# Where TensorE's dense pieces stand in the HGRN head: five of 32 moved behind the norm sum

## The reference, cut to what matters

```python
proj = u @ P['w_in'][l]                       # columns for A, B, C and the gates G
# HGRN2, per head, chunk by chunk
o_inter = jnp.einsum('bhtk,bhkv->bhtv', q_c * jnp.exp(g_cum), s)
att = jnp.einsum('bhtk,bhsk,bhtsk->bhts', q_c, k_c, dec)
o = o_inter + jnp.einsum('bhts,bhsv->bhtv', att, v_c)
s = jnp.exp(g_last)[:, :, 0, :, None] * s + jnp.einsum('bhsk,bhsv->bhkv', k_c * jnp.exp(g_last - g_cum), v_c)
# after all chunks
o = o * lax.rsqrt(jnp.mean(o * o, axis=-1, keepdims=True) + RMS_EPS) * norm_g
out = o * jax.nn.silu(gz)
# merge
ga, gb, gc = jnp.split(jax.nn.sigmoid(pg), 3, axis=-1)
merged = ga * (oa @ proj_a) + gb * (ob @ proj_b) + gc * (oc @ proj_c)
```

## Time and profile before

| | |
|---|---|
| median of three runs | 2198.53 us (2196.08 to 2199.20) |
| the profiled execution | 2198.53 us, span 2196.7 us |
| mean granted TensorE clock | 0.993 |
| TensorE busy, matmuls | 2106.6 us, 96% |
| VectorE, ScalarE busy | 1311.3 us, 817.7 us |
| HGRN heads in the span | about 647 to 773 us and 1728 to 1854 us |

### The profile page before, as it was taken

The page is one execution under the profiler, slowest core; times in us unless marked ns, Lnnn a source line. Parts: engine busy times, 40 slices in busy tenths (PEclk is TensorE's granted clock), DMA queues, the critical chain, the costliest instruction groups (busy, mean ns, idle before and its releaser), DMA issues.

```text
span 2196.7 us, 30927 instructions
## 1 busy us (share of the span) xinstructions
PE 2106.6 (96%) x12624; PEld 1856.3 (85%) x12624; DVE 1311.3 (60%) x1947; ACT 817.7 (37%) x931; POOL 35.9 (2%) x72
## 2 busy tenths in 40 slices
PE   5999999999999989999999999999999999999998
PEld 5999997777766688999989998977777666989998
DVE  4664376776556674665366644766764576656643
ACT  3554352122143144554355534412112323445532
POOL 0000000000000000000000000000000000000000
PEclk9999999999999999999999999999999999999999
DMA  4444421111132242444434443211111323324442
GB/s 167 153 153 156 170 96 45 68 49 68 44 107 106 100 154 96 146 148 159 160 137 148 150 160 134 102 39 51 67 54 65 111 107 127 137 96 152 152 155 100
DMA packets 38067, 252.13 MB, mean 115 GB/s; under 512 B 4720, under 2 KB 4912, under 8 KB 9424
## 3 DMA queue, kind: packets, MB, share of 16 engines
q1 hardware_dynamic: 33120, 234.60, 30.1%
q0 software_dynamic: 4848, 16.13, 2.0%
HBM read 242.05 MB, written 8.67 MB: 114 GB/s over the span
## 4 chain that ended last, share of the span: by engine, by line
PE 85%; DVE 8%; ACT 2%; DVEq 2%; issue 1%; DMA 1%; ACTq 0%; POOLq 0%
PE dps L580 42%; PE dps L532 15%; PE dps L487 9%; DVE tmp L1203 2%; PE mx L680 2%; PE mx L674 2%; PE mx L682 2%; ACT tmp L891 1%; PE mx L549 1%; PE mx L560 1%; PE mx L487 1%; PE mx L789 1%; DVEq L1632 1%; PE mx L825 1%; DVE ho L1203 1%
## 5 line engine op out<-in xcount | busy, mean ns | idle before, releaser
L532 PE MATMUL dps<-u,raw 128*128 128x320 f32 x1536 | 478.0, 439 | 0.0
L1200 DVE TENSOR_TENSOR wlo<-raw,whi 128x2048 fp32r<-128x2048 f32 x136 | 311.7, 2292 | 259.9 <-ACT whi L891 254.9
L580 PE MATMUL dps<-uh,whi 128*128 128x320 f32 x1408 | 433.2, 308 | 34.7 <-DVE wlo L1200 25.5
L580 PE MATMUL dps<-uh,wlo 128*128 128x320 f32 x1408 | 436.0, 310 | 0.0
L580 PE MATMUL dps<-ul,whi 128*128 128x320 f32 x1408 | 434.7, 309 | 0.0
L891 ACT ACTIVATE whi<-raw 128x2048 fp32r<-128x2048 f32 x138 | 262.8, 1905 | 389.4 <-PE dps L580 380.5
L532 PEld LDWEIGHTS dps<-u,raw 128*128 128x128 f32 x1536 | 269.5, 190 | 89.2 <-issue 13.7
L580 PEld LDWEIGHTS dps<-uh,whi 128*128 128x128 f32 x1408 | 266.4, 189 | 37.6 <-issue 31.2
L580 PEld LDWEIGHTS dps<-ul,whi 128*128 128x128 f32 x1408 | 265.6, 189 | 1.3 <-issue 0.2
L580 PEld LDWEIGHTS dps<-uh,wlo 128*128 128x128 f32 x1408 | 266.5, 189 | 0.0
L580 PE MATMUL dps<-hfh,whi 128*128 128x320 f32 x704 | 221.1, 314 | 0.0
(11 more groups left out here) (297 smaller groups left out, 3026.1 us busy)
## 6 DMA issues: line engine op xcount, KB each, us to landing
raw<-in_wstream SPq DMA_DIRECT2D x220, 1024.0 KB, 4.8
hs<-in_st_hgrn POOLq DMA_DIRECT2D x8, 512.0 KB, 6.2
out_o_hgrn<-hs POOLq DMA_DIRECT2D x8, 512.0 KB, 2.9
sw<-in_smallw POOLq DMA_DIRECT2D x2, 1024.0 KB, 5.2
ss<-in_st_rwkv POOLq DMA_DIRECT2D x8, 256.0 KB, 3.9
out_o_rwkv<-ss POOLq DMA_DIRECT2D x8, 256.0 KB, 2.3
x<-in_xT SPq DMA_DIRECT2D x4, 320.0 KB, 4.3
out_yT<-x SPq DMA_DIRECT2D x4, 320.0 KB, 2.2
```

What stands on the lines that cost most here:

```text
L532: m = pe.matmul(dps[:, 2 * s + c, 0:T], w[:, k, c * P:(c + 1) * P], u[:, k, :], start=k == 0, stop=k == KD - 1, skip_group_check=True)
L580: m = pe.matmul(dps[:, 2 * half + c, 0:T], w[:, k, c * P:(c + 1) * P], v[:, k0 + k, :], start=first and k == 0 and i == 0, stop=last and k ...
L1200: return nc.vector.tensor_tensor(out, a, b, op)
```

## The change

Of the 32 pieces of each head, the five that stood singly or in a pair between the state products and the end of the output products are issued at the end of the head, behind the norm sum. The number of pieces, their order among themselves, and every wait and semaphore are as before. The 17th piece, the first of the second block, now comes behind `o_done`.

```diff
                 pe.matmul(mx[:, 2, P:2 * P], kt3[:, 1, :], vt3[:, 1, :], start=True, stop=True)\
                     .then_inc(S["hst1_done"], 1)
-                dense_part(1)
                 pe.wait_ge(S["hb_ready"], n + 1)
                 for j in range(2):
                     m = pe.matmul(mx[:, j, :], kt3[0:CH, 2, :], hvb[0:CH, 4 * j:4 * j + 4, :], start=True, stop=True)
                 m.then_inc(S["hst_done"], 1)
-                dense_part(2)
                 pe.wait_ge(S["hst1_ready"], n + 1)
                 pe.wait_ge(S["hs_loaded"], n * 16 + 16)
...
                 for b in range(NB):
-                    if b % 4 == 0:
-                        dense_part(1)
                     t0 = TP + b * TS
                     m = pe.matmul(mx[:, 3, t0:t0 + TS], hs[:, b, :], qps[1][:, t0:t0 + TS], start=False, stop=b == NB - 1)
                 m.then_inc(S["o_done"], 1)
                 dense_part(3)
                 pe.wait_ge(S["osq_ready"], n + 1)
                 pe.matmul(mx[:, 2, 0:T], ones, osq, start=True, stop=True).then_inc(S["om_done"], 1)
-                dense_part(8)
+                dense_part(13)
```

## The result

The changed kernel takes 2209.74 us (median of 4 runs, 2209.49 to 2210.34) against 2197.33 before (4 runs, 2196.08 to 2199.20): a ratio of 1.0056, 95% interval 1.0039 to 1.0074. It is slower by 12 us. Measured once more in a later comparison it took 2207.89 against 2198.16, 1.0042 (1.0026 to 1.0057). The profiled execution took 2208.12 us with a span of 2206.3, 9.6 us more than before, so that is what the traces have to account for.

The account below looks back on a forecast made before the run. It took TensorE's queue length plus its few waits to bound the kernel. Pace 0, new waits 0, first wait -2.1, second wait +2.1 and clock +1.6 on 2198.5 gave 2200.1 us, range 2195.8 to 2202.4.

Parts of the forecast that it names:

- The clock at that pause: Pause behind the fourth heads: both pauses become the longer kind, one more clock fall than now, +1.6 us.
- a sign of being wrong: Distance from head to head: a change of over 0.3 us would show the prediction wrong.
- the one on the slower side: L794 becomes a wait if VectorE's chain is over 0.62 us later; 2203.1 us at 1.2 later; chance 0.05.
- The pace: Each head: 2.60 to 2.98 us saved in the stretch against 2.69 added at the end; taken as 0.
- the lower of the two readings of the 0.10: Stretch from L784: the 0.10 us after a change of rows stays without the pieces, so it is not saved.
- The waits that come closer: Ahead of L789 and L794: 0.48 and 0.62 us of cover left, so no new wait, cost 0.
- What comes earlier: `o_done` and its chain come 2.7 us earlier; VectorE's lead ends waiting at L1614, so nothing is gained.
- The last head: Behind the fourth head: first wait of 1.05 us goes, third half's grows from 2.37 to 3.42; gain 0.
- 1: Behind the last head: first wait goes, second grows, layer 1 keeps its clock; 2198.5 us; chance 0.36.
- 2: Behind the last head: the 1.05 us gain is kept in each layer; 2196.4 us; chance 0.05.
- 3: Level loop: VectorE's lead carries through five later levels of each head, saving 15 us; 2184 us; chance 0.04.
- 4: Ahead of L794: VectorE's chain comes later than its 0.62 us cover; 2203.1 us at 1.2 later; chance 0.05.

Follow-up runs that it names:

- e7: Changed kernel's order plus an unread identity-times-constants product in each of the five gaps, against the kernel before: 2219.98 us against 2197.74, ratio 1.0095.
- e5: Kernel before with the five pieces moved behind `o_done` but ahead of the norm sum: 2204.52 us against 2197.74, ratio 1.0034.
- e8: Kernel before with the five pieces moved into levels 3 to 6 and ahead of L779: 2195.89 us against 2197.74, ratio 0.9988.
- e1: Kernel before with the change made only in the fourth head of each layer: 2202.48 us against 2198.15, ratio 1.0025.
- e2: Kernel before with the change made only in the first three heads of each layer: 2203.91 us against 2198.15, ratio 1.0028.
- e9: Kernel before with three pieces, from ahead of L789, L794 and L783, moved into levels 4 to 6: 2189.50 us against 2197.74, ratio 0.9960.
- e3: Kernel before with only the two single pieces around L802 moved to the head's end: 2202.08 us against 2198.15, ratio 1.0023.
- e6: Kernel before with all five pieces in one clump between L789 and L794: 2203.89 us against 2198.16, ratio 1.0026.
- e4: Kernel before with only the three pieces ahead of L794 moved to the head's end: 2201.67 us against 2198.15, ratio 1.0021.
- e11: Second measurement of the kernel with three pieces moved into levels 4 to 6, against the kernel before: 2186.07 us against 2198.16, ratio 0.9942.
- e10: Three pieces in levels 4 to 6, the one left ahead of L794 moved ahead of the first L802, against the kernel before: 2187.69 us against 2198.16, ratio 0.9951.

## Why the prediction was wrong

*The step that failed is the one named "The clock at that pause".* It asked for the clock only where TensorE stands still, and took it as given, 1.00, inside the heads. There it fell in four of eight, 1.7 us each, 6.8 us in the profile, and these heads came 1.7 us further apart, where the prediction had named 0.3 as a sign of being wrong. The rule of the Trainium skill that I leaned on (TensorE: Matmul & The Clock Gate, "What's actually happening": the slow state is the default, activity releases it) speaks of activity, and I read it as the absence of pauses. The trace speaks against my reading: in the window ahead of the fall shown above TensorE is busy throughout. It does not speak against the rule's wording, and e7, where added wide products take most of the falls away, agrees with it. No rival had it either; the one on the slower side was a wait.

*In the same step, the size at the pause was too small.* I forecast one fall more, +1.6. Measured from steps in the profile, the two places lose 3.8 us more: both have a fall, as forecast, and each lasts longer than the one fall before the change (0.72 over 12 us against 0.86).

The other steps held. *The pace:* the stretch from L784 to the dense row took 7.96 us and takes 5.27, so taking the pieces out saves 2.69 a head, exactly what they cost at the end; 31.35 us a head against 31.36 before, so 0, as the lower of the two readings of the 0.10 had it: L788 to L792 is 1.91, L798 follows L795 0.36 us behind, the 0.10 behind a change of rows stays. *The waits that come closer:* no idle ahead of L788 or L792. *What comes earlier:* VectorE's lead ends in its wait at L1614 of before:

```profile
682.09 0.44 DVE L1610 COPY_PREDICATED ho<-cst,mx 128x256 f32<-128x256 uint32 x1 [2.83 <-PE mx L768]
```

2.83 us against 0.15, forecast 2.8; the level loop gained nothing. *The last head:* first wait gone, second one at 3.63 against 3.42 forecast, gain kept 0; the chain starts at the last piece. *The rivals:* 1 falls with the clock, 2 with the second wait, 3 with the wait at L1610, 4 since L792 follows at once. The sum of the parts other than the clock was 0 and measured 0; the whole error is the clock inside the heads and the size of its falls behind them.

That the falls come from the stretch without dense pieces is shown by the runs together. The bare stretch brings them without the longer pause and the long row (e5), a wide product in each gap takes them from four to one with the order of the change kept (e7), and a kernel with the stretch bare behind full levels has them in every head (e8). Over all profiles, heads with the bare stretch hold a fall in 25 cases of 40 (both profiles of the changed kernel, e1, e2, e5, e8), heads with their pieces as before in none of 16 (before, e1, e2). And all 35 falls in heads, those behind a pause left out, begin between 0.8 us ahead of the last small product's start and 1.2 us behind it. What is not shown is which products of the stretch count how much: with some of the pieces in it there are falls in three heads, two, one or none of eight (three in e9, two in e3 and e6, one in e4 and e11, none in e10).

## What to carry to other kernels

Wide instructions between small matmuls may be holding the clock and not hiding a wait, so before they are moved out of a thin run, look at what is left of the run and, afterwards, at the granted clock in windows of a few us behind it: the page's slices average a fall away, and a busy TensorE says nothing. If such work is to be moved, the profitable place is where TensorE waits for another engine (0.54 us of work put into a level cost 0.03 here), and enough of it has to stay behind: five pieces moved there gained nothing clear of noise, three gained 8 to 12 us.

## What the hardware showed that I had not expected

The granted clock fell to 1.2 GHz with TensorE 3.00 of 3.00 us busy ahead of the fall, after products of 128, 512 (64 rows), 64 and 8 columns. Products of the identity with constants in the gaps brought it down to one head in eight, against four with nothing there and none with the dense pieces there. And the falls sat in the same four heads in two profiles of the changed kernel, though not in two profiles of another kernel (e9 and e11), and the instructions of the stretch are the same in every head.
